# Attention scores of both branches behind each other, and two sets of score banks in token tiles 0 to 3

## The reference

```python
s = einsum('bgrqd,bgnd->bgrqn', qi, ck) * scale      # compressed keys, 63 of them
p_c = masked_softmax(s, cmp_end <= t)
...
s = einsum('bgrqd,bgqkd->bgrqk', qi, ksel) * scale   # selected blocks: with top 16 of 16, all keys up to t
p_s = masked_softmax(s, smask)
...
s = einsum('bgrqd,bgkd->bgrqk', qi, kwi) * scale     # window of the last 512 keys
p_w = masked_softmax(s, wmask)
o = g0 * p_c @ cv + g1 * p_s @ v_slc + g2 * p_w @ v_win
```

## Time and profile before

| | us |
|---|---|
| median of 3 runs | 1595.13 (1593.61 to 1596.15) |
| the profiled execution | 1594.84 |
| its span, first to last instruction | 1593.0 |
| TensorE busy | 1554.4 |
| VectorE busy | 894.0 |
| ScalarE busy | 537.2 |
| granted TensorE clock, mean share of full | 0.992 |

### The profile page before, as it was taken

How to read it: one execution, slowest core, us unless ns; L and a number is a source line. 1 busy time by engine, 2 the same in 40 slices (tenths; PEclk the granted TensorE clock), 3 DMA queues, 4 the chain that set the end, 5 groups by cost and what they waited for, 6 DMA issues and landing times.

```text
span 1593.0 us, 21511 instructions
## 1 busy us (share of the span) xinstructions
PE 1554.4 (98%) x8238; PEld 1261.9 (79%) x8238; DVE 894.0 (56%) x1561; ACT 537.2 (34%) x936; POOL 79.7 (5%) x126
## 2 busy tenths in 40 slices
PE   8999999998899999999999999999999999999997
PEld 6888888897666666788888888888888888888885
DVE  7832456446777676443455555656555565556332
ACT  6112222246777677422212211222112221223221
POOL 0111222220000000000000000000000000000000
PEclk9999999998999999999999999999999999999998
DMA  6433342380000000601211111121111111122011
GB/s 230 133 106 126 100 145 95 115 257 18 25 18 14 14 1 10 242 1 42 78 40 58 61 40 40 40 79 40 40 40 55 64 40 40 40 80 106 27 40 40
DMA packets 53239, 110.57 MB, mean 69 GB/s; under 512 B 13104, under 2 KB 22320, under 8 KB 53168
## 3 DMA queue, kind: packets, MB, share of 16 engines
q1 hardware_dynamic: 45744, 85.47, 16.1%
q0 software_dynamic: 7424, 24.12, 4.5%
HBM read 89.65 MB, written 19.92 MB: 69 GB/s over the span
## 4 chain that ended last, share of the span: by engine, by line
PE 95%; DVE 2%; issue 2%; ACT 1%; DMA 0%; DVEq 0%; POOLq 0%; POOL 0%; SPq 0%; ACTq 0%
PE ps L1520 29%; PE ps L1139 15%; PE ps L1141 15%; PE ps L1140 15%; PE ps L1246 5%; PE ps L1425 5%; PE ps L1382 2%; PE ps L1383 2%; PE ps L1507 1%; PE ps L1291 1%; PE ps L1239 1%; PE ps L1144 1%; PE ps L1386 1%; PE ps L1205 1%; PE ps L1380 0%
## 5 line engine op out<-in xcount | busy, mean ns | idle before, releaser
L2069 DVE TENSOR_TENSOR h<-h,ps 128x512 f32<-128x512 f32 x336 | 224.4, 686 | 137.8 <-PE ps L1141 136.2
L1520 PE MATMUL ps<-htl,wuh 128*128 128x512 f32 x672 | 206.9, 389 | 0.0
L1520 PE MATMUL ps<-hth,wul 128*128 128x512 f32 x672 | 206.9, 389 | 0.0
L1520 PE MATMUL ps<-hth,wuh 128*128 128x512 f32 x672 | 206.8, 389 | 0.0
L1139 PE MATMUL ps<-wh,xth 128*128 128x512 f32 (+1 forms) x448 | 175.2, 391 | 7.6 <-DVE wl L1654 7.6
L1141 PE MATMUL ps<-wh,xtl 128*128 128x512 f32 (+1 forms) x448 | 169.2, 378 | 0.0
L1140 PE MATMUL ps<-wl,xth 128*128 128x512 f32 (+1 forms) x448 | 168.7, 377 | 0.0
L1520 PEld LDWEIGHTS ps<-hth,wul 128*128 128x128 f32 x672 | 126.1, 188 | 26.2
L1520 PEld LDWEIGHTS ps<-hth,wuh 128*128 128x128 f32 x672 | 126.1, 188 | 26.2
L1520 PEld LDWEIGHTS ps<-htl,wuh 128*128 128x128 f32 x672 | 126.1, 188 | 26.2
L1083 ACT ACTIVATE ffh<-ffa 128x1024 fp32r<-128x1024 f32 x22 | 23.3, 1061 | 358.3 <-DVE ffa L2096 358.3
(11 more groups left out here) (249 smaller groups left out, 2593.6 us busy)
## 6 DMA issues: line engine op xcount, KB each, us to landing
wuraw<-in_w_up SPq DMA_DIRECT2D x44, 512.0 KB, 4.9
wraw<-in_w_in SPq DMA_DIRECT2D x48, 256.0 KB, 3.3
proj_d<-stage POOLq DMA_DIRECT2D x48, 256.0 KB, 2.3
wdraw<-in_w_down SPq DMA_DIRECT2D x22, 512.0 KB, 3.6
rin<-proj_d POOLq DMA_DIRECT2D x20, 256.0 KB, 4.7
xraw<-in_xt SPq DMA_DIRECT2D x16, 256.0 KB, 6.0
owraw<-in_w_out SPq DMA_DIRECT2D x8, 512.0 KB, 5.5
h<-in_x SPq DMA_DIRECT2D x1, 4096.0 KB, 16.6
```

Source lines behind the costliest of these rows:

```text
L1520: mm = nc.tensor.matmul(ps[:, 2 * part + half, :], w_, x_[:, k, half * 512:(half + 1) * 512], start=(k == 0 and i == 0), stop=(k == NK - 1 ...
L2069: nc.vector.tensor_tensor(hh, hh, ps[:, 4 + o_ % 4, :], ALU.add).then_inc(dn_add, 1)
```

## The change

TensorE now makes both steps of a head behind each other, at the end of every odd slot (`qk_pair`). VectorE takes both maxima at the start of the even slot. ScalarE's exponentials are placed by `exp_places`: in tiles 0 to 3 both at the end of the odd slot; in later tiles both in the even slot, one in the middle of its copies and one at the end (the first head's both at the end). In tiles 0 to 3, where a score set fits one bank, even heads use banks 0 and 2 and odd heads banks 1 and 3 (`score_bank`), and scores wait for the exponential four steps before (`apart`); the compressed scores stay in bank 3, so step 1 still waits for the step two before, and step 3, which goes to bank 3 too, waits for `csub`.

```diff
@@ -509,6 +509,15 @@
             done = (2 * RG + 1) * v + 2 * RG - 1
             return done + br if v // G >= WIN_T else done + 1 + (br > 0)
 
+        def apart(t):
+
+            return 4 if t < WIN_T else 2
+
+        def score_bank(t, i):
+
+            r_, br = divmod(i, 2)
+            return 2 * br + (r_ % 2 if t < WIN_T else 0)
+
         plan = [("split_q", 0), ("turn_q", 0)] + [st for slot in slots for st in slot]
         turns_of = {st: n for n, st in enumerate(st for st in plan if st[0].startswith("turn"))}
         outs_of = {(v, j): n for n, (v, j) in enumerate(st[1:] for st in plan if st[0] == "output")}
@@ -936,7 +945,8 @@
                 act.wait_ge(nb_done, n + 1)
                 if v >= 2:
                     act.wait_ge(tr_full, turns_of["turn_p", v - 2, len(key_tiles(v - 2)) - 1] + 1)
-                s_, pr = ps[:, 2 * br:2 * br + 2, :].rearrange("p a n -> p (a n)"), prob[:, v % 2, r_]
+                at = score_bank(t, i)
+                s_, pr = ps[:, at:at + 2, :].rearrange("p a n -> p (a n)"), prob[:, v % 2, r_]
                 m, q = n % 4, n // 2 % 4
                 if br == 0:
                     nc.scalar.activation(pr[:, 0:(t + 1) * P], s_[:, 0:(t + 1) * P], ACT.Exp, bias=nb[:, m:m + 1],
@@ -978,6 +988,19 @@
                 act.wait_ge(pv_done, outs_of[v, len(key_tiles(v)) - 1] + 1)
                 nc.scalar.activation(nsah[:, 2 * g_:2 * g_ + 2, t * P:(t + 1) * P],
                                      ps[:, 7, 0:2 * P].rearrange("p (a n) -> p a n", a=2), ACT.Copy).then_inc(nsah_done, 1)
+
+            def exp_places(n, length):
+
+                v, i = divmod(n, 2 * RG)
+                if v >= NV:
+                    return {}
+                if v // G < WIN_T:
+                    return {length: [i - 1, i]} if i % 2 else {}
+                if i % 2:
+                    return {}
+                if i == 0:
+                    return {length: [0, 1]}
+                return {(length + 1) // 2: [i], length: [i + 1]} if length > 1 else {length: [i, i + 1]}
 
             for e in range(2):
                 k_copy(e)
@@ -1003,11 +1026,12 @@
             act.wait_ge(cv_done, CV0 + 1)
             nc.scalar.activation(cv[:], ps[0:NCMP, 1, P:2 * P].rearrange("p (g d) -> p g d", g=G), ACT.Copy).then_inc(cvc_done, 1)
             for n, slot in enumerate(slots):
-                for st in slot:
+                at_ = exp_places(n, len(slot))
+                for m, st in enumerate([*slot, ("end",)]):
+                    for i in at_.get(m, ()):
+                        exponentials(n // (2 * RG), i)
                     {"split_q": q_split_high, "turn_q": q_turned, "turn_p": p_high, "turn_ret": ret_high,
                      "close": nsa_high}.get(st[0], skip)(st)
-                if n < 2 * RG * NV:
-                    exponentials(*divmod(n, 2 * RG))
                 if n in OW_SLOTS:
                     ow_high(OW_SLOTS[n])
 
@@ -1353,17 +1377,23 @@
 
                 n, (t, g_), (r_, br) = 2 * RG * v + i, divmod(v, G), divmod(i, 2)
                 pe.wait_ge(tr_h, turns_of["turn_q", v] + 1)
-                if n >= 2:
+                if n >= apart(t):
+                    pe.wait_ge(exp_done, n - apart(t) + 1)
+                if i == 1 and t < WIN_T and n >= 2:
                     pe.wait_ge(exp_done, n - 1)
                 if i == 1 and v:
                     pe.wait_ge(csub_done, CSUB0 + v)
+                if i == 3 and t < WIN_T:
+                    pe.wait_ge(csub_done, CSUB0 + v + 1)
+                if i == 2 and v == 0:
+                    pe.wait_ge(cvc_done, CVC0 + 1)
                 q_ = aqt[:, v % 2, r_ * P:(r_ + 1) * P]
                 w0 = 0 if br == 0 else max(0, t - WIN_T)
                 width = (t + 1 - w0) * P
                 c0 = P + r_ * HD
                 for c in range(0, width, 512):
                     w = min(512, width - c)
-                    bank = 2 * br + c // 512
+                    bank = score_bank(t, i) + c // 512
                     at = w0 * P + c
                     joint = br and c
                     masks = []
@@ -1395,6 +1425,10 @@
                         mm = nc.tensor.matmul(sc_, ident_b[:], cmp_b[:, t], start=False, stop=True)
                 mm.then_inc(qk_done, 1)
 
+            def qk_pair(v, r_):
+                qk(v, 2 * r_)
+                qk(v, 2 * r_ + 1)
+
             def p_turn(st):
                 v, j = st[1:]
                 br, _, at, w = key_tiles(v)[j]
@@ -1448,12 +1482,12 @@
             pe.wait_ge(cks_done, 1)
             pe.wait_ge(aks_done, 8)
             pe.wait_ge(akx_done, 8)
-            qk(0, 0)
+            qk_pair(0, 0)
             for n, slot in enumerate(slots):
                 for st in slot:
                     {"turn_q": q_turn, "turn_p": p_turn, "output": pv, "turn_ret": ret_turn}.get(st[0], skip)(st)
-                if n + 1 < 2 * RG * NV:
-                    qk(*divmod(n + 1, 2 * RG))
+                if n % 2 and n + 1 < 2 * RG * NV:
+                    qk_pair(*divmod((n + 1) // 2, RG))
 
 
             def out_product(n, k):
@@ -1888,7 +1922,8 @@
                 n, t, br = 2 * RG * v + i, v // G, i % 2
                 dve.wait_ge(qk_done, n + 1)
                 m = n % 4
-                s_ = ps[:, 2 * br:2 * br + 2, :].rearrange("p a n -> p (a n)")
+                at = score_bank(t, i)
+                s_ = ps[:, at:at + 2, :].rearrange("p a n -> p (a n)")
                 if br == 0:
                     nc.vector.reduce_max(nb[:, m:m + 1], s_[:, 0:(t + 1) * P], AX_X, negate=True).then_inc(nb_done, 1)
                     return
@@ -1897,7 +1932,7 @@
                     nc.vector.reduce_max(nb[:, m:m + 1], s_[:, 0:w], AX_X, negate=True).then_inc(nb_done, 1)
                     return
                 c_ = cmpst[:, v % 2]
-                scores = s_[:, 5 * P:5 * P + RG * HD].rearrange("p (r n) -> p r n", r=RG)[:, :, 0:NCMP]
+                scores = ps[:, 3, P:P + RG * HD].rearrange("p (r n) -> p r n", r=RG)[:, :, 0:NCMP]
                 maximum = mark(nc.vector.reduce_max(c_[:, C_MAX], scores, AX_X, negate=True))
                 nc.vector.reduce_max(nb[:, m:m + 1], s_[:, 0:w], AX_X, negate=True).then_inc(nb_done, 1)
                 dve.wait_ge(dve_chain, maximum)
@@ -1989,8 +2024,9 @@
             for n, slot in enumerate(slots):
                 behind = n // 2 - 1
                 due = 0 <= behind < RG * NV
-                if n < 2 * RG * NV:
+                if n % 2 == 0 and n < 2 * RG * NV:
                     row_max(*divmod(n, 2 * RG))
+                    row_max(*divmod(n + 1, 2 * RG))
                 if n % 2 == 0 and due:
                     v_, head = divmod(behind, RG)
                     inverted = invert_sum(v_, head)
```

## The result

The changed kernel takes 1617.36 us (median of 4 runs, 1616.0 to 1618.33), the kernel before 1594.97 (4 runs): ratio 1.0135, 95% interval 1.0123 to 1.0147. It is slower, as forecast, but by 22.4 us where I had 5.7, outside the range. The profiled execution took 1618.26 us.

What follows compares the result with a forecast made beforehand. TensorE bounds the kernel, busy 1554.4 of 1593.0 us. Starts, groups 2 to 4, groups 0 and 1, late tiles and clock: 4.2-1.4-1.5+2.7+1.7 = +5.7 on 1594.84 gives 1600.5 us; own range 1598.3 to 1604, with rivals 1591 to 1606.

Steps and rivals of the forecast that it cites:

- The new wait at a group's start: First turn of the finished group's probabilities waits for the last normalization behind the new group's maxima: 2.24 us at group 6.
- groups 5 to 7: At these starts, the new wait less retention turns and idle time saved: 1.3, 1.9 and 1.0, together +4.2 us.
- groups 2 to 4: New waits of 1.8 to 2.0 us, but two bank sets let the ring's idle time vanish: together -1.4 us.
- Groups 0 and 1: First two groups: with two sets, scores stand behind each other and idle time goes: -1.5 us.
- Clock: New waits of about 2 us bring TensorE one further stretch at half clock: +1.7 us, bounds 0 and 8.5.
- the 1.51 us at 638: TensorE's wait after the last group, forecast to go because the last head's scores are made a slot earlier.
- Rival C: Clock falls at most group starts: five low stretches, 4.0+8.5 = +12.5 us, 1607 us; chance 0.10.
- Late tiles: Groups 8 to 15: later first turns sum to 4.2 us, less the wait at the end: +2.7 us.
- inside a group I cost it at 0: Late tiles, one bank set: pairing was to cost nothing between starts; without cover, up to one window exponential per head.
- the odd groups: Late odd groups: retention's low part, no longer behind the window maximum, saves some or all of the start's delay.
- The cover named: Late tiles: slots' own turns and outputs, with ScalarE's slack (537 of 1593 us), were to hide paired exponentials.
- Rival B: Faster: denser scores keep the clock full in groups 0 and 1, ring idle gone: -5.5 us, 1589 us; chance 0.20.

Runs made afterwards that it cites:

- filler kernel: Changed kernel plus six 512-column matmuls ahead of the first turn at the starts of groups 2 to 7, their result overwritten: 1612.5 us, ratio 1.0112.
- fastest kernel: Kernel before with pairs and two bank sets in tiles 0 to 3 alone, last head's normalization ahead of the window maximum at group starts 1 to 7: 1587.38 us.
- late-only kernel: Kernel before with pairs in tiles 4 to 7 alone, tiles 0 to 3 as before: 1609.01 us, ratio 1.0089.
- two sets alone: Kernel before with two sets of score banks in tiles 0 to 3 and nothing paired: 1590.81 us, ratio 0.9978.

## Why the prediction was wrong in size

The sum was +2.1 of idle time up to T0 of group 8 (its wait among it), +1.9 behind it and +1.7 of clock. The traces give +5.2, +8.3 and +8.6, so 3.1, 6.4 and 6.9 us more.

*The new wait at a group's start: right.* The chain, row by row, was 2.24 and is 2.23 us. For groups 5 to 7 the sum had 2.2-0.5, 2.2 and 2.2-0.5, 5.6 us, before idle time saved; they are 1.63+2.23+1.82 = 5.7. For groups 2 to 4 it had 5.1; they are 1.83+1.43+2.03 = 5.3.

*Groups 0 and 1: a gain taken where there was a loss.* With the idle time saved in groups 2 to 4 (6.4), at the starts of groups 5 to 7 (1.5) and in groups 0 and 1 (1.5) I had 9.4 us going. Outside T0's waits, idle time fell from 11.4 (11.97 less 0.6 for T0 of group 8) to 4.7 us, by 6.7. That is 2.7 of the miss, and nearly all of it lies ahead of T0 of group 2: there idle time rose from 2.6 to 3.6 us instead of falling by 1.5. Behind it the gain was 7.7 us, as good as the 7.9 forecast. The prediction saw that a group's last exponential is waited for again, but took the gain whole. In group 0 scores wait for `csub` and for window exponentials:

```profile
369.44 0.30 PE L1412 MATMUL ps<-keys_s,aqt 128*128 128x128 f32 x1 [1.01 <-DVE csub L1942]
...
374.21 0.45 PE L1412 MATMUL ps<-keys_s,aqt 128*128 128x128 f32 x1 [1.10 <-ACT prob L958]
```

*Clock: the main failed step.* "I take one further low stretch, +1.7" leaned on the 1.51 us at 638, which had left the clock alone. Other waits of that length and more did not: there were five more stretches in all, 20 us more at the lower level, 8.6 us lost. Rival C's mechanism is what happened, at five starts of fifteen, with its bound of 8.5, but its other terms were mine and too small. The filler kernel is the test that the low clock costs time and is not a mere companion of the waits: with the waits as long at five of its six starts, 7.2 us came back. The Trainium skill, TensorE: Matmul & The Clock Gate, section "A second HAM failure mode: psum-queue depth-cycling", ties frequent brief pauses in one kernel to a clock that swings and to lost throughput. Of the lost throughput the trace agrees. Frequency alone does not explain it here: fewer, longer pauses (six of 1.4 to 2.2 us) swung it more than the kernel before, whose 12.0 us of early idle time lay in pieces of at most 0.9.

*Late tiles: "inside a group I cost it at 0" failed.* T0's waits for normalizations from group 8 on rose from 3.1 to 8.8 us, and the 1.51 at the end went, as forecast. But the forecast let the odd groups save 2.2 us of waits for the retention's low part, and these rose instead, from 1.9 to 3.7; waits for copies `ptf` rose from 0.9 to 3.2. The cover named, ScalarE's slack (537 of 1593 us), is an average; what counts is which instruction stands ahead of which. With T0's waits as before (3.3 us) the late part still lost 9.0 us: 7.1 of idle time and 1.9 of busy time. Its waits for `retl` (1.86, 2.40, 2.20) are 4.6 us more than before and those for `ptf` (1.73 the longest) 3.1 more, less the 1.51 at the end. Neither place tried for the window exponential takes them away without new ones, so that this queue order is their cause is read from the trace and not shown by a kernel without the loss.

*Rival B* wanted about 7 us from the early groups. Once T0's wait is gone, the fastest kernel has 6.5 of them, its clock there 0.95 against 0.93, and 1587.4 us against B's 1589. In the changed kernel itself B's mechanism did not show: the low stretch in groups 0 and 1 was as long as before (13.7 us both times); in the fastest kernel it was 10.2 us. That its time comes near B's is in part luck, since it has the late tiles unchanged.

*Open:* why the clock falls at one wait and not at another. The 1.51 us at 638 had no low clock behind it, nor had the changed kernel's waits of 1.82, 1.57, 1.55, 2.02 and 1.62 us at groups 7 to 11; it fell there once more, behind 1.94 us at 640. And the late-only kernel had low stretches at 388 to 392 and 398 to 406 us, in a part ordered as before, where the kernel before had none, and two sets alone had them at 387 to 401 us. So part of the clock's behaviour in groups 2 and 3 may not come from T0's waits; with the mended order no run's profile has a low stretch there.

## What to carry to other kernels

When scores are gathered, look at what else stands in the consumer's queue behind them: here four VectorE instructions ahead of the last normalization, at the seven starts of tiles 0 to 3, cost 18 us, and moving them behind it turned a loss of 1.35% into 0.2%, or, with the late tiles left alone, into a gain of 0.5%. In this kernel gathering paid only where a second set of buffers existed; with one set, producers ask a slot earlier for what consumers give no sooner (1616 against 1587 us). And price a new idle wait on TensorE in the middle of dense work at more than its length: here 13.6 us of idle time came with 8.6 us of slower work, though only some of the waits brought it. A wait removed is also worth less than its length if another stands behind it: 5.5 us less of T0's waits in the late tiles made them 1.2 us shorter.

## What was not expected of the hardware

Adding 36 matmuls to the critical engine made the kernel 4.9 us faster by the medians, since they kept the granted clock up. And the same program's runs differ by where the clock falls: 1610 us at a mean clock of 0.991 and 1615 at 0.988; for the two-set kernel eight of ten runs took 1590.5 to 1592.8 us at 0.991 or 0.992 and two 1594.2 and 1595.1 at 0.989.
